# Opening order, prologue residual loads and two weight loads of an eight-core hybrid encoder, moved

## What is computed

```python
def even_mixer(h, ...):            # layer 0
    z = h @ w_in                                   # 1024 -> 1536: a, gate, p
    ya = conformer_conv(a, gate, conv_w, ...)      # a * sigmoid(gate), conv of 31, layernorm, silu
    yb = multiscale_pool(p, pool_w, pool_scale)
    return jnp.concatenate([ya, yb], axis=-1) @ w_out
def odd_mixer(h, ...):             # layer 1
    z = h @ w_in                                   # c, u, v
    yc = fourier_mix(c, fourier_w)                 # real 2-D DFT, then a matmul per head
    yd = spatial_gating(u, v, ...)                 # u * (W_s layernorm(v) + b), chunks of 128
    return jnp.concatenate([yc, yd], axis=-1) @ w_out
def swiglu(h, w_gate, w_up, w_down):               # 1024 -> 2816 -> 1024
    return (jax.nn.silu(h @ w_gate) * (h @ w_up)) @ w_down
```

## Time and profile before

| | |
|---|---|
| three runs, median (lowest to highest) | 2523.09 us (2523.01 to 2526.21) |
| the profiled execution, its own time | 2526.24 us |
| its span on the slowest core, core 2 | 2524.9 us |
| spans of the eight cores | 2516.0 to 2524.9 us |
| PE busy on core 2 | 2492.2 us, 99% of the span |
| DVE, ACT, POOL busy | 35%, 26%, 16% |
| PE waits on core 2: for `wgu` loads | 5.5 us in 2 waits |
| PE waits on core 2: for DVE's `hb` | 3.8 us in 3 waits |

### The profile page before, as it was taken

How to read it: one execution, slowest core, us unless ns; L and a number is a source line. 1 busy time by engine, 2 the same in 40 slices (tenths; PEclk the granted TensorE clock), 3 DMA queues, 4 the chain that set the end, 5 groups by cost and what they waited for, 6 DMA issues and landing times.

```text
span 2524.9 us, 37754 instructions; the slowest of 8 cores (2516.0 to 2524.9 us)
## 1 busy us (share of the span) xinstructions
PE 2492.2 (99%) x12432; PEld 1183.1 (47%) x12582; DVE 890.7 (35%) x1474; ACT 658.3 (26%) x1198; POOL 408.9 (16%) x709
## 2 busy tenths in 40 slices
PE   8999999999999999999999999999999999999998
PEld 5445444444444444444444574444444444444444
DVE  4487466222222222211234872322223222222212
ACT  4436341131111121111155752211111111111111
POOL 3212132011101110010034521210111011101101
PEclk9999999999999999999999999999999999999999
DMA  8976899777766996567473297993577457644523
GB/s 177 190 134 139 149 176 162 160 165 125 118 142 118 168 156 143 105 76 103 126 116 98 34 208 131 171 158 99 116 130 115 119 121 129 114 121 92 79 47 101
DMA packets 310220, 323.71 MB, mean 128 GB/s; under 512 B 146177, under 2 KB 268305, under 8 KB 309906
## 3 DMA queue, kind: packets, MB, share of 16 engines
q0 software_dynamic: 123488, 121.41, 37.6%
q1 hardware_dynamic: 181506, 195.40, 30.2%
q10 hardware_dynamic: 5040, 4.47, 0.6%
HBM read 325.70 MB, written 79.69 MB: 161 GB/s over the span
## 4 chain that ended last, share of the span: by engine, by line
PE 95%; DMA 3%; issue 1%; DVE 1%; ACT 0%; POOL 0%; ACTq 0%; DVEq 0%; POOLq 0%; SPq 0%
PE ps L171 95%; DMA wgu<-ffn_wgu 1%; DMA xin<-x 1%; DMA xres<-xr 0%; DMA xr<-x 0%; DVE bst L1028 0%; DVE hb L378 0%; DVE xr L469 0%; POOL ssb L358 0%; ACT BIG L1050 0%; DVE svr L1420 0%; ACT hb L372 0%; ACT BIG L1077 0%; POOL rs L358 0%; ACT hbp L372 0%
## 5 line engine op out<-in xcount | busy, mean ns | idle before, releaser
L171 PE MATMUL ps<-BIG,wgu 128*128 128x512 bf16 x5632 | 1227.9, 379 | 5.5 <-DMA wgu<-ffn_wgu 5.5
L171 PEld LDWEIGHTS ps<-BIG,wgu 128*128 128x128 bf16 x5632 | 550.9, 98 | 669.4 <-issue 8.6
L171 PE MATMUL ps<-wd,gT 128*128 128x512 bf16 (+1 forms) x2775 | 604.5, 377 | 3.3
L495 DVE TENSOR_TENSOR gT<-tmp,ps 128x512 bf16<-128x512 f32 x352 | 242.1, 688 | 809.6 <-PE ps L171 788.8
L171 PEld LDWEIGHTS ps<-wd,gT 128*128 128x128 bf16 x2838 | 277.7, 98 | 330.4
L493 ACT ACTIVATE tmp<-ps 128x512 f32<-128x512 f32 x352 | 209.3, 595 | 768.0 <-PE ps L171 726.8
L185 POOL DMA_DIRECT2D wgu<-ffn_wgu x176 | 134.5, 764 | 857.4 <-PE ps L171 828.8
L171 PE MATMUL ps<-w_in,BIG 128*128 128x512 bf16 (+1 forms) x1075 | 227.9, 364 | 3.7 <-ACT BIG L407 1.7
L372 ACT ACTIVATE hb<-xr 128x1024 bf16<-128x1024 f32 x80 | 84.6, 1058 | 547.7 <-DVE xr L469 266.9
L171 PE MATMUL ps<-w_out,BIG 128*128 128x512 bf16 x968 | 219.7, 379 | 4.4 <-ACT BIG L1077 1.4
L356 POOL TENSOR_TENSOR ssb<-ssb,epsd 128x1 f32<-128x1 f32 x159 | 34.4, 216 | 1003.0 <-ACT hb L372 631.4
(11 more groups left out here) (149 smaller groups left out, 1162.3 us busy)
## 6 DMA issues: line engine op xcount, KB each, us to landing
wgu<-ffn_wgu POOLq DMA_DIRECT2D x176, 512.0 KB, 7.8
xr<-xr SPq DMA_DIRECT2D x59, 512.0 KB, 5.1
xr<-xres SPq DMA_DIRECT2D x32, 512.0 KB, 5.8
xnat<-xr SPq DMA_DIRECT2D x32, 512.0 KB, 4.6
out<-xr SPq DMA_DIRECT2D x31, 512.0 KB, 3.3
xr<-x SPq DMA_DIRECT2D x30, 512.0 KB, 7.8
xres<-xr SPq DMA_DIRECT2D x30, 512.0 KB, 5.4
xr<-xnat SPq DMA_DIRECT2D x27, 512.0 KB, 7.9
```

The lines of the kernel that those rows point to most:

```text
L171: ins = self.nc.tensor.matmul(o, lhsT=l, rhs=r, start=st, stop=sp)
L495: k.op(dve, lambda e: e.tensor_tensor(out=gT[:, j, tg * 512:(tg + 1) * 512], in0=tmp[:], in1=ps[:, bl[1], :], op=ALU.mult), reads=[d_tmp, ...
```

## The change

It does three things. **Opening:** 18 warm-up matmuls in three places instead of 6 in two; the squares of tiles 2 and 3 directly behind each other; the transpose of tile 1 evacuated by ACT and not DVE; the loads in the order WG1, x4, WA1, x5, x6, x7 and not x4, WG1, x5, WA1, x6, x7; `val(0,0)` and `val(1,0)` ahead of `gate(2,0)`. **Prologue of layer 0:** three more residual slots, `xpz` in bytes that z tiles 2 and 3 held and two `xpy` where z tiles 4 to 7 were, so that tiles 5, 6 and 7 are loaded without waiting for a store. **Odd mixer:** the output-weight load stands behind `v_rs1(31)`, the down-weight load behind `sv(31)`.

```diff
-        def tr_in(t):
+        def tr_in(t, eng):
             nrm.scale(t)
-            nrm.tr_pe(t, ident, d_ident, t % 2)
-
+            nrm.tr_pe(t, ident, d_ident, eng)
+
+        warmup(6)
         n_stat(0)
         w_load(WA, 0)
         n_stat(1)
-        tr_in(0)
-        warmup(3)
+        tr_in(0, 0)
+        warmup(7)
+        n_stat(2)
+        n_stat(3)
+        w_load(WG, 1)
+        tr_in(1, 0)
+        warmup(5)
         n_load(4)
-        n_stat(2)
-        tr_in(1)
-        warmup(3)
-        w_load(WG, 1)
-        n_stat(3)
+        w_load(WA, 1)
         n_load(5)
-        w_load(WA, 1)
         n_load(6)
         n_load(7)
         w_load(WP, 0)
         w_load(WP, 1)
         gate(0, 0)
         gate(1, 0)
-        tr_in(2)
-        tr_in(3)
+        tr_in(2, 0)
+        tr_in(3, 1)
+        val(0, 0)
+        val(1, 0)
         gate(2, 0)
         n_stat(4)
-        val(0, 0)
-        val(1, 0)
         gate(3, 0)
...
-                if t + len(op.xr.s) < 8:
+                if t + len(op.xr.s) < 8 and t + len(op.xr.s) not in op.st:
                     op.load(t + len(op.xr.s))
...
                 xpt, d_xpt = k.buf("xp", 108 * KB, [D], F32, 2)
-                for n in range(2):
-                    xpro.s.append((xpt[:, n], d_xpt[n]))
+                xpz, d_xpz = k.buf("xpz", 68 * KB, [D], F32, 1)
+                xpro.s.extend([(xpt[:, n], d_xpt[n]) for n in range(2)] + [(xpz[:, 0], d_xpz[0])])
+                for n in range(3):
                     op.load(3 + n)
...
             if i == 0:
                 ln_norm(3)
+                xpz, d_xpz = k.buf("xpy", 72 * KB, [D], F32, 2)
+                for n in range(2):
+                    xpro.s.append((xpz[:, n], d_xpz[n]))
+                    op.load(6 + n)
...
         v_rs1(NT - 1)
+        wo, d_wo = load_w_out("od_w_out", 168 * KB)
         f_first(6)
...
             if n == 3:
                 sv_upto(NT)
+                wdt = k.lazy("wd", 108 * KB, [D], BF16, NJ)
+                for j in range(10, 18):
+                    dma_runs(pool, wdt[0][:, j, :], T["ffn_wd"][1, j], writes=[wdt[1][j]])
         gbc3, gscale3 = load_gbc(3, 202 * KB, True)
         f_mix(1)
-        wo, d_wo = load_w_out("od_w_out", 168 * KB)
...
-            if h == 1:
-                wdt = k.lazy("wd", 108 * KB, [D], BF16, NJ)
-                for j in range(10, 18):
-                    dma_runs(pool, wdt[0][:, j, :], T["ffn_wd"][1, j], writes=[wdt[1][j]])
```

## The result

The change takes 2532.21 us (median of 13 executions) against 2523.44 of the kernel before (13). The ratio is 1.0029, 95% interval 1.0020 to 1.0038: slower by 7.3 us, 5.0 to 9.6. The forecast, 2523.3 and "no change", was wrong.

What follows compares the result with a forecast made beforehand. PE, 99% busy, bounds the kernel; only idle or slow-clock PE time on the last core counts. Core 5, last after +3.15 - 4.8, lies 2.95 under old core 2: 2526.24 - 2.95 = 2523.3, no change; range 2518.3 to 2527.0.

Steps and rivals of the forecast that it cites:

- Opening, +2.7 and +3.15: Opening: later x tile 5 delays tile 6's transpose, costing 2.7 us on core 2 and 3.15 on core 5.
- x5 lands where WA1 did: Opening loads: x tile 5 lands at WA1's old date, 30.9 on core 2 (3.4 us later), 33.2 on core 5.
- my upper bound: Opening: up to +5 us if x tile 4's new wait adds its own delay to that of x tile 5.
- the same restart in the prologue: Layer-0 prologue, core 5: time lost at the slow clock after the wait, 1.6 us, counted in the 4.8 gain.
- PE's warm-ups, 0: Opening: extra warm-ups and faster first gates stay hidden behind the wait for WA0; price 0, bounds -1.7 and +1.
- Prologue, -0.9 and -4.8: Layer-0 prologue: earlier residual loads remove the late transpose's wait, gaining 0.90 us on core 2, 4.8 on core 5.
- Next late would be the third `wgu`: Layer-0 prologue: the third up weight would be late next, but also comes earlier with the loads out of its way.
- Odd mixer, -7.1 on core 2: Odd mixer: earlier output and down weights remove layer 1's up-weight waits (0.46, 4.99) and slow restart (1.69), 7.1 us.
- my only price for the earlier issue: Odd mixer: four issues hold POOL for 3.08 us, delaying `sv` multiplies at most 1.5; taken as 0.
- rule on two-port copies: Odd mixer: DVE copies taking both ports block GpSimd's DMA descriptors; w_out would start a few us later, still before 1451.
- The sum over cores: Whole kernel: core 2 at 2519.6, core 5 at 2521.95 and last, core 0 at 2518.7; time 2523.3.
- Rival 3: Layer 1: up-weight stall stays because SP's queue shares the DMA engines, opening also later; 2528.0 to 2528.5, chance 0.10.

Runs made afterwards that it cites:

- e10: Kernel before plus the new opening, x tile 4 loaded late (behind WG1) but x tile 5 still ahead of WA1; ratio to before 1.0010.
- e2: The change with the residual loads of the layer-0 prologue put back as before; ratio to the kernel before 1.0013.
- e3: The change with the odd mixer's output-weight and down-weight loads put back at their old places; ratio to the kernel before 1.0017.
- e12: The unaltered change run once more as a control; ratio to the kernel before 1.0053.
- e1: The change with its opening put back as before, prologue and odd mixer still changed; ratio to the kernel before 1.0004.
- e7: Kernel before plus only the early prologue slot `xpz` (tile 5), without the slots for tiles 6 and 7; ratio to before 1.0002.
- e16: Kernel before plus the early prologue slot `xpz` (tile 5) and one `xpy` (tile 6); ratio to before 1.0003.
- e11: Kernel before plus the new opening, x tile 4 ahead of WG1 as before but x tile 5 late, behind WA1; ratio to before 1.0004.
- e6: Kernel before plus the odd mixer's change alone (output-weight and down-weight loads both earlier); ratio to before 1.0000.
- e13: Kernel before with only the odd mixer's output-weight load moved forward; ratio to before 0.9997.
- e9: Kernel before plus the new opening with x tiles 4 and 5 loaded early as before, and `xpz` alone; old odd mixer; ratio to before 0.9995.
- e14: Kernel before with only the eight down weights moved forward, now ahead of the output weight; ratio to before 1.0031.

## Why the prediction was wrong, step by step

- **Opening, +2.7 and +3.15: right in mechanism, and in the mean nearly in size.** "x5 lands where WA1 did" held in the mean of the cores (31.0 against 31.4, 3.4 later than before, as forecast), but not core by core: 31.7 against a forecast of 30.9 on core 2, 30.0 against 33.2 on core 5. O is 3.1 us later than in the trace of before, and 3.6 in the means of the kernels with the new and with the old opening. Not counted was the clock: in the waits ahead of tile 4's transpose and copy PE fell to 1.2 GHz on six of the eight cores (mean clock 0.50 to 0.74 in the lower of the windows 28 to 33 and 33 to 38 us), up to 2 us, though I counted the same restart in the prologue. Tile 4's own wait, my upper bound, is real (e10), but does not add to tile 5's: 1.9 and 4.4 alone, 3.6 together (O of the change, e2, e3 and e12, 47.21 in the mean, less 43.66). Core 5 became 1.8 later, core 2 5.7, and all eight lost.
- **PE's warm-ups, 0**: right. The faster clock is there and hidden.
- **Prologue, -0.9 and -4.8: this step failed, and it turned the sign of the sum.** The wait for tile 7 went, as forecast. But "Next late would be the third `wgu`; the loads taken out of its way make it earlier too" is wrong. The loads were not taken out of its way, they were put ahead of it: tiles 6 and 7 had been issued at 243.0 and 251.4 us, behind the first pair of weights (238.5, core 4 of before), and are issued at 236.0 and 238.2 now, the first of them 2 us ahead of the pair (237.8, core 0 of e1). Only for tile 5 was the sentence right (e7). O to P is 253.00 in the mean of the change, e1, e3 and e12, and 250.23 in the nine kernels with the old prologue: +2.8 where I had a gain, and the mean span of e2 says the same (2.4 to 3.0). I had read from the earlier trace rows that in layer 1 a full pair of queues makes weights late, and did not ask the same of layer 0.
- **Odd mixer, -7.1 on core 2: mechanism right, size not.** The stall went from nearly all cores. But 5.45 us was the worst of eight cores of one execution (four of them waited for nothing); in nine kernels with the old order W to F loses 0.85 in the mean of the cores. Since core 5 was the last in my sum, the error cost nothing. The pause of PE was not foreseen; my only price for the earlier issue was POOL's, and it was 0 (3.08 us for four issues, as before). The Trainium skill's rule on two-port copies ("SBUF — State Buffer", "Who interferes with whom") would have made these issues drag; the row shows no drag.
- **The sum over cores.** Taking cores 2 and 5 as the ones that matter was the wrong frame for a change that moves every core: the last core was one that had no wait before. Nor was core 3 in the sum, the second slowest at 2524.0. In means over the cores of the traces the parts give +3.6, +2.8 and -0.15, 6.2; the mean span is 7.1 longer, 7.7 in e12, and the slowest core 7.3 (5.0 to 9.6). Rival 3's time was nearest (2528.0 to 2528.5 against 2530.7, which is 2523.44 + 7.3), and the two queues did share the engines as it says, but in layer 0. The range ended at 2527.0, short of that rival's own times.

## What to carry over

A load moved forward has to be charged to whatever it now stands in front of: list, for each queue that shares the engines, what will be late next, with its date of need and its slack, before booking the gain. Here two loads of 512 KB cost 2.8 us of mean time and one cost little or nothing (e16, 0.7 us of mean span, good to 1.0), since a slack of some 4 us hid it. And a cost or gain read off one core of one execution is a draw: take the mean over the cores, and if there are more executions, over these.

## What was not expected of the hardware

- With loads from POOL and SP both waiting, POOL's queue moved 0.19 MB in 5 us beside 0.54 MB of SP's, against 0.58 MB alone.
- Equal waits do not cost PE's clock equally: in one run (e11) a wait of 3.06 us left core 2 at 2.4 GHz, and one of 3.07 us left core 6 at 1.2 GHz.
- With the output weight issued at the end of the odd mixer, PE stops in the middle of the same `m,A` matmuls some 20 us later, mostly with no releaser in the trace (in e1, e6 and e13 the copy to `Y` is named on some cores). It occurs in all eight kernels that issue it early, 0.4 to 1.8 us and once 3.0 (e12, core 6), on four to eight of their cores; of those that issue it late only in e9 at this place, on two cores. With DMA engines as full but the down weights first it is not there (e14's core 0: share 1.21 at 1455 to 1460), so full engines alone are not the cause.
- What PE waits for can be read from the DMA rows: its own instructions. Every 7 to 14 us one packet of 16 KB comes in a queue of the kind "instruction". Core 7 of e13, 1464 to 1465 us (packets, MB, share of the engines, so that it took 1.2 us):

```profile
q8 instruction: 1, 0.02, 7.6%
```

It runs from 1464.91 to 1466.13, and PE, out of work since 1466.15, goes on at 1467.94. So it is everywhere: all 46 pauses of 0.4 us or more among the `m,A` and `gcs,Y` matmuls between 1455 and 1480 us, in 11 kernels, end 1.05 to 1.83 us (1.48 in the mean) behind the landing of such a packet. In the eight kernels nearly all pauses begin at one and the same point of the program (14.8 us behind M, or 16.15 with the old opening), and of the 16 cores that do not pause there, 15 had the packet 1.3 us or more before PE came to that point. The rows do not say whose instructions a packet holds; that they are PE's is inferred from these dates. Why the packet lands too late with this order of loads, and not in e14, is open.
